# The long convolution's spectral products, ordered by feature tile instead of by spectrum half

## The reference

```python
def two_sided_fft_conv(u, h_fwd, h_bwd, bias):
    L = u.shape[1]
    kern = jnp.concatenate([h_fwd, jnp.zeros((1, h_fwd.shape[1]), F32), h_bwd[:0:-1]], axis=0)
    spec = jnp.fft.rfft(uf, n=2 * L, axis=1) * jnp.fft.rfft(kern, n=2 * L, axis=0)[None]
    y = jnp.fft.irfft(spec, n=2 * L, axis=1)[:, :L]
    return (y + uf * bias.astype(F32)).astype(u.dtype)

def hyena_mixer(h, ...):
    u = centred_depthwise_conv(h @ w_in + b_in, short_w, short_b)
    v, x1, x2 = jnp.split(u, 3, axis=-1)
    z = x1 * two_sided_fft_conv(v, filt[:, 0, 0], filt[:, 0, 1], filt_bias[0])
    z = x2 * two_sided_fft_conv(z, filt[:, 1, 0], filt[:, 1, 1], filt_bias[1])
    return z @ w_out + b_out
```

## Time and profile before

| | us |
|---|---|
| median of 3 runs | 3072.62 |
| the profiled execution's time | 3072.21 |
| its span, from the first to the last instruction | 3070.4 |
| TensorE busy | 2749.7 (90%) |
| VectorE busy | 1200.4 (39%) |
| ScalarE busy | 683.9 (22%) |

### The profile page before, as it was taken

The page is one execution under the profiler, slowest core; times in us unless marked ns, Lnnn a source line. Parts: engine busy times, 40 slices in busy tenths (PEclk is TensorE's granted clock), DMA queues, the critical chain, the costliest instruction groups (busy, mean ns, idle before and its releaser), DMA issues. The chain is left out here.

```text
span 3070.4 us, 37233 instructions
## 1 busy us (share of the span) xinstructions
PE 2749.7 (90%) x15352; PEld 1686.8 (55%) x15352; DVE 1200.4 (39%) x2257; ACT 683.9 (22%) x1422; POOL 20.1 (1%) x27
## 2 busy tenths in 40 slices
PE   8888999998998989867699999999898977988887
PEld 7656687885576667655463344333576755222223
DVE  5455433334365746575620111121536543111113
ACT  4344233332110111100211111111316631101101
POOL 0000000000000000000000000000010000000000
PEclk9999899997999999978799999999898989999998
DMA  4430423234110101010249999999331034999996
GB/s 177 144 124 7 159 82 110 82 110 159 52 52 1 55 24 41 24 55 0 111 157 375 353 346 344 344 340 345 123 139 46 2 137 165 415 427 429 427 428 256
DMA packets 56137, 550.17 MB, mean 179 GB/s; under 512 B 8199, under 2 KB 18823, under 8 KB 23208
## 3 DMA queue, kind: packets, MB, share of 16 engines
q1 hardware_dynamic: 55976, 547.93, 45.9%
HBM read 545.81 MB, written 2.10 MB: 178 GB/s over the span
## 5 line engine op out<-in xcount | busy, mean ns | idle before, releaser
L2623 PE MATMUL experts_pg_l<-ring,moe_xe_l 128*64 128x512 f32 x1024 | 269.5, 604 | 43.1 <-DMA ring<-in_moe_gu 37.7
L2623 PE MATMUL experts_pu_l<-ring,moe_xe_l 128*64 128x512 f32 x1024 | 263.5, 592 | 0.0
L2815 DVE SCALAR_TENSOR_TENSOR residual<-experts_psc,mod,residual 128x512 f32<-128x512 f32 (+1 forms) x101 | 71.9, 715 | 449.1 <-PE experts_psc L2704 375.0
L2648 PE MATMUL experts_py_l<-ring,experts_turn_l 128*64 128x512 f32 x976 | 223.6, 600 | 24.3 <-DMA ring<-in_moe_down 23.0
L1820 PE MATMUL hyena_lat<-normed,ring 128*128 128x512 f32 x384 | 172.2, 602 | 8.5 <-PEq L415 7.2
L2623 PEld LDWEIGHTS experts_pg_l<-ring,moe_xe_l 128*64 128x64 f32 x1024 | 63.4, 136 | 170.3 <-issue 101.9
L2648 PEld LDWEIGHTS experts_py_l<-ring,experts_turn_l 128*64 128x64 f32 x976 | 66.6, 137 | 163.0 <-issue 122.5
L2623 PEld LDWEIGHTS experts_pu_l<-ring,moe_xe_l 128*64 128x64 f32 x1024 | 74.3, 137 | 145.5 <-issue 145.5
L1820 PEld LDWEIGHTS hyena_lat<-normed,ring 128*128 128x128 f32 x384 | 73.1, 192 | 94.3 <-issue 93.2
L2807 DVE TENSOR_TENSOR experts_y_low<-experts_py_l,experts_y_whole 64x512 fp32r<-64x512 f32 x64 | 44.1, 689 | 196.9 <-ACT experts_y_whole L2765 134.8
L2796 DVE SCALAR_TENSOR_TENSOR experts_hid_l<-experts_act_l,moe_gate_rows,experts_pu_l 128x512 f32<-128x512 f32 x32 | 23.9, 747 | 238.8 <-ACT experts_act_l L2748 238.8
(11 more groups left out here) (551 smaller groups left out, 4999.4 us busy)
## 6 DMA issues: line engine op xcount, KB each, us to landing
ring<-in_moe_gu SPq DMA_DIRECT2D x128, 2048.0 KB, 10.1
ring<-in_moe_down SPq DMA_DIRECT2D x61, 2048.0 KB, 10.0
ring<-in_ada_w SPq DMA_DIRECT2D x24, 2048.0 KB, 7.8
ring<-in_w_up SPq DMA_DIRECT2D x8, 2048.0 KB, 7.7
ring<-in_w_down SPq DMA_DIRECT2D x8, 2048.0 KB, 7.7
ring<-in_hy_w_in SPq DMA_DIRECT2D x4, 2048.0 KB, 8.1
ring<-in_w_in SPq DMA_DIRECT2D x3, 2048.0 KB, 15.0
hyena_win<-table_window SPq DMA_DIRECT2D x4, 1536.0 KB, 7.5
```

The lines of the kernel that those rows point to most:

```text
L2623: last = nc.tensor.matmul((pg_l, pu_l)[m][64 * half:64 * half + 64, :], xe_l[:, e, k, :], w[:, kk, m, FH * half:FH * (half + 1)], start=(k ...
L2648: last = nc.tensor.matmul(py_l[64 * half:64 * half + 64, :], turn_l[:, c, i, :], columns(c, FH * half, FH), start=(f == 0), stop=(f == KD ...
L2815: nc.vector.scalar_tensor_tensor(out=x[:, d, c0:c0 + n], in0=banks[bank][:, 0:n], scalar=gate[j][:, d:d + 1], in1=x[:, d, c0:c0 + n], op0= ...
```

## The change

`products` handles a tile of 128 features, both halves of the spectrum, and then that tile's four sums, before it goes on to the next tile. `combined` is raised once for each tile, and `back` waits for it once for each tile. The twelve products keep 768 elements each, now as 6 rows of 128 out of 256; the sums are 8 of 3 × 128 instead of 4 of 768.

```diff
--- before.py
+++ after.py
@@ -1754,7 +1754,7 @@
         even_kept = st.counter("hy_even_kept", 24 * TURNS)
         convolved = st.counter("hy_convolved", NP * TURNS)
         taps_made = st.counter("hy_taps_made", 12 * TURNS)
-        combined = st.counter("hy_combined", 2 * TURNS)
+        combined = st.counter("hy_combined", 4 * TURNS)
         gated = st.counter("hy_gated", 2 * TURNS)
         win_loaded = st.counter("hy_win_loaded", 32 * TURNS)
         tab_loaded = st.counter("hy_tab_loaded", 64)
@@ -1863,8 +1863,8 @@
                         last.then_inc(ip_done.handle, 1)
 
                 def back(it, o):
-                    pe.wait_ge(combined.handle, it * 2 + combined.at(o + 1))
                     for j in range(2):
+                        pe.wait_ge(combined.handle, it * 4 + combined.at(2 * o + j + 1))
                         bl, bc = take(it, "back", 2 * o + j)
                         for b, table, tiles, n in ((bl, tables["idft_l"], (0, 1), 256), (bc, tables["idft_c"], (2,), P)):
                             for par in range(2):
@@ -2045,21 +2045,22 @@
                         dve.wait_ge(taps_made.handle, it * 12 + taps_made.at(6 * o + t + 1))
 
                 def products(it, link, o):
-                    for s in range(2):
-                        A, B = flat(ab[:, 0, s]), flat(ab[:, 1, s])
-                        Pc, Qs = flat(pq[:, 0, s]), flat(pq[:, 1, s])
-                        p1, p2 = (t1, t2) if s == 0 else (t3, t4)
-                        nc.vector.tensor_tensor(p1[:], A, Pc, ALU.mult)
-                        link(nc.vector.tensor_tensor(p2[:], B, Qs, ALU.mult))
+
+                    for j in range(2):
+                        tile = slice(j * P, (j + 1) * P)
+                        A, B, Pc, Qs = [v[:, a].rearrange("p s f n -> p (s f) n")[:, :, tile] for v in (ab, pq) for a in range(2)]
+                        p1, p2 = [t[:].rearrange("p (f n) -> p f n", n=P) for t in ((t1, t2), (t3, t4))[j]]
+                        nc.vector.tensor_tensor(p1, A, Pc, ALU.mult)
+                        link(nc.vector.tensor_tensor(p2, B, Qs, ALU.mult))
                         nc.vector.tensor_tensor(A, A, Qs, ALU.mult)
                         link(nc.vector.tensor_tensor(B, B, Pc, ALU.mult))
                         link(nc.vector.tensor_tensor(B, A, B, ALU.add))
-                        link(nc.vector.tensor_tensor(A, p1[:], p2[:], ALU.subtract))
-                    lo, hi = [flat(ab[:, a, 0]) for a in range(2)], [flat(ab[:, a, 1]) for a in range(2)]
-                    nc.vector.tensor_tensor(flat(pq[:, 0, 0]), lo[0], hi[0], ALU.add)
-                    nc.vector.tensor_tensor(flat(pq[:, 0, 1]), lo[0], hi[0], ALU.subtract)
-                    nc.vector.tensor_tensor(flat(pq[:, 1, 0]), lo[1], hi[1], ALU.subtract)
-                    nc.vector.tensor_tensor(flat(pq[:, 1, 1]), lo[1], hi[1], ALU.add).then_inc(combined.handle, 1)
+                        link(nc.vector.tensor_tensor(A, p1, p2, ALU.subtract))
+                        lo, hi = [[ab[:, a, s, :, tile] for a in range(2)] for s in range(2)]
+                        nc.vector.tensor_tensor(pq[:, 0, 0, :, tile], lo[0], hi[0], ALU.add)
+                        nc.vector.tensor_tensor(pq[:, 0, 1, :, tile], lo[0], hi[0], ALU.subtract)
+                        nc.vector.tensor_tensor(pq[:, 1, 0, :, tile], lo[1], hi[1], ALU.subtract)
+                        nc.vector.tensor_tensor(pq[:, 1, 1, :, tile], lo[1], hi[1], ALU.add).then_inc(combined.handle, 1)
 
                 def gates(it, link, o):
                     for j in range(2):
```

## The result

The changed kernel takes 3043.11 us (median of 4 runs, 3041.84 to 3044.01), the kernel before 3073.32 us (4 runs) in the same comparison: a ratio of 0.990 with an interval of 0.9888 to 0.9911. The forecast was 3041.7 us, with 3036 to 3048.5 as its range.

The account below looks back on a forecast made before the run. TensorE is busy 90% of the span, so only its idle and slow-clock time can give much. Five block gains sum to 30.7 us, giving 3041.5 from the profiled 3072.2 or 3041.9 from the median: 3041.7 us, range 3036 to 3048.5.

Parts of the forecast that it names:

- Which blocks wait: Inverse transform, 8 places: 3 covered by projections (order 0, full turns), 5 on TensorE's path, waiting 50.9 us in all.
- When the tiles are ready: From the products' start T on VectorE: tile 0 at T + 7.72, tile 1 at T + 15.30; before, both at T + 15.02.
- the larger estimate: Four extra sums on VectorE at a fixed 0.15 us each: 0.6 us a block instead of 0.28, 1.6 us in all five.
- The runs of 128: VectorE's products with operands in six runs of 128 elements: no cost taken; the other end was 9 us in all.
- Rival 5: VectorE's tile 1 work slows while TensorE loads tile 0's weights from pq: at factor 2.2, 15 us lost, 3087; chance 0.01.
- The start of tile 0 in a full turn: Order 1: TensorE leaves projection 5 at T + 9.02, transforms tile 0 to T + 13.36, then waits 1.94 us for tile 1.
- The tail: Order 1: the output product follows 7.10 us after tile 1's transform starts, as before, with tile 1's gating covered.
- Tile 0 in the last turn: Transform starts at T + 7.72 at the lower clock, ends at T + 14.7 or T + 13.8, ahead of tile 1.
- The gain of a block, b − 0.28: Each waiting block gains tile 0's old transform time b less 0.28: 6.89, 5.56, 5.74, 6.73 and 5.82 us.
- Rival 2: The new gap slows tile 1 in all three full turns, costing 6.0 to 8.5 us: 3047.7 to 3050; chance 0.15.
- rival 1: Slow stretches vanish behind the shorter gaps, 4.4 us more gained: 3037.3; chance 0.12.
- The shift reaches the end: Later loads wait for the program and move with the stage, so the whole 30.7 us was taken.

Follow-up runs that it names:

- experiment 2: The changed kernel with order 0 of the three full turns put back to the old form of `products`: 3045.88 us, ratio 0.9911 to the kernel before.
- experiment 8: The changed kernel with one more unread 768-element VectorE operation ahead of tile 1's products in all 8 blocks: 3047.7 us, ratio 0.9905 to the kernel before.
- experiment 5: The changed kernel with 4 unread matmuls in the gap ahead of tile 1 in the full turns: 3039.69 us, ratio 0.9893 to the kernel before.
- 4: The changed kernel with the output product begun on gated tile 0 while VectorE gates tile 1: 3033.6 us, ratio 0.9871 to the kernel before.
- experiment 6: The changed kernel with unread matmuls ahead of tile 1, the output product and the last turn's taps transform: 3037.44 us, ratio 0.9885 to the kernel before.
- the first run of 7: The changed kernel with the output product begun early and unread matmuls ahead of tile 1 and the taps' transform: 3027.0 us, ratio 0.9849 to the kernel before.
- experiment 3: The kernel before with unread matmuls ahead of each inverse transform that waits: 3057.54 us, ratio 0.995 to the kernel before.

## Why the prediction was right

- *Which blocks wait.* Three covered, five on the path: the blocks of the two traces and experiment 2 show it, and in experiment 8 0.87 us more of VectorE's time move tile 1 by 0.88 us in the five and by nothing in the three.
- *When the tiles are ready.* Forecast T + 7.72 and T + 15.30; measured 7.72 and 15.30 in the last turn. In the full turns tile 1 starts at T + 15.38, 0.08 us later than its signal would allow by the last turn's figures; these are the 0.06 and 0.07 us by which the first and the third turn fell short. The eight sums cost 0.28 us a block, not the 0.6 of the larger estimate.
- *The runs of 128.* They cost nothing. The line of L2053 and those of the sums, ns min/median/max:

```profile
L2053 DVE TENSOR_TENSOR hyena_t<-hyena_ab,hyena_pq x16: 948/954/958, 865.8 to 1396.3; 128x768 f32<-128x768 f32 x16
...
L2060 DVE TENSOR_TENSOR hyena_pq<-hyena_ab x16: 558/559/559, 871.5 to 1402.0; 128x384 f32<-128x384 f32 x16
...
L2063 DVE TENSOR_TENSOR hyena_pq<-hyena_ab x16: 547/550/553, 872.9 to 1403.4; 128x384 f32<-128x384 f32 x16
```

  The sums take the 0.56 us that was read between the forms of 256 and 512 elements, 0.47 apart. Rival 5 (VectorE slowed while TensorE loads weights from pq) fell by the same rows: the products of tile 1 that run beside tile 0's transform take 0.95 to 0.96 us.
- *The start of tile 0 in a full turn.* Forecast T + 9.02, measured 8.85: the 3.62 us of the projection's last group is an end that overlaps the next group. The transform still ended at T + 13.36 as forecast (948.71 − 2.02 = 946.69), so the early start gave and cost nothing. The gap is 2.02 us, not 1.94, because tile 1 starts at T + 15.38.
- *The tail.* 7.10 us from tile 1 to the output product; measured 7.09 (948.71 to 955.80). Behind its wait tile 1's transform takes 4.61 us to its end (955.80 − 2.48 − 948.71), over the 4.5 that was named as a sign of being wrong. That bound was too tight: 0.1 us of it is the first group behind a wait (3.71 us against 3.62), not a slow clock.
- *Tile 0 in the last turn.* Forecast to end at T + 14.7 and T + 13.8. It ended at T + 15.3 in order 0, with no wait left ahead of tile 1, and at T + 15.1 in order 1 (0.20 us of wait): the slow stretch was longer than in the old rows, the slack of 0.6 us in order 0 was used up, and that it cost nothing is luck.
- *The gain of a block, b − 0.28.* Four of five came within 0.1 us. The one step that missed is the clock behind the new gap, taken as 0: in the second turn tile 1 ran 1.69 us longer. Rival 2 thus held in one turn of three, in both profiles of the changed kernel and in that of experiment 2. Against it two output products that had been slow ran at full speed, part of rival 1. The forecast was for such a mixture. Between the blocks 5.0 us were gained and as much lost; the loss, 1.7 us in the first turn and 3.4 in the second in the filters and projection 4, stood in no term of the forecast, so that the two cancel is luck.
- *The shift reaches the end.* Of the 28.7 us 25.7 did (30.4 less the 4.7 that came ahead of the convolution). The first products of the expert stage still started 32.9 us earlier (1545.04 against 1577.89), so the loads came with the program, as the earlier trace rows let expect. Of the 3.0 us some 0.6 went by 2303 us of the old trace (32.8 us of shift left there) and the rest behind it, mostly in the second expert feed-forward; the cause is open. The sum of 30.7 was therefore 2.0 us too high in the blocks, mainly by the slow tile 1. That the 3041.7 us came so near 3043.11 is in part luck: 4.7 us came from ahead of the convolution and 3.0 went behind it.
- The Trainium skill's rule of gaps over about 3 us ("TensorE: Matmul & The Clock Gate", "Why this matters for your kernels") would have kept the clock up behind 2.0 and 2.5 us. The trace disagrees: tile 1 behind 2.02 us took 5.40 us in the second turn, the output product behind 2.48 us 3.60 in experiment 5. Nor does length alone decide: behind 2.90 us in experiment 8 tile 1 was fast in all three full turns, and slow once, behind 2.39, in the last. What came before seems to matter. Five profiles have nothing in the gap ahead of tile 1 (both of the changed kernel, experiments 2, 4 and 8), so fifteen such gaps in full turns. Tile 1 was slow in three, and these are the three where the turn had already lost 3.4 us before it (69.2 us from order 0's T to order 1's; elsewhere 67.5 or 65.8, a loss of 1.7 or none). Why was not tried.

## What to carry to other kernels

Where one engine makes a whole result and the next waits for all of it, order the work by what the consumer takes first and signal each piece. The gain is at most the consumer's time for the first piece, and only in the places where the wait is really on the path: read each occurrence, since three of eight here were covered. A long wait may bring slow-clock time right behind it; a third of this gain was that. Then look at the next joint of the chain, where the same step may be open again.

## What was not expected of the hardware

TensorE's granted clock fell to the lower level (1.2 GHz) without a gap worth the name. In the changed kernel's first turn the filters (L1840) have one gap of 0.48 us; projection 4 behind them takes 8.83 us, and about 7.1 us before. Timeline, then (fields as under the result) two stretches of the changed kernel and the like one of the kernel before, where the clock did not fall:

```profile
893.76 4.88 PE L1840 MATMUL hyena_spec<-hyena_w,hyena_h 64*128 64x256 f32 x20
899.12 1.13 PE L1840 MATMUL hyena_spec<-hyena_w,hyena_h 64*128 64x256 f32 x4 [0.48 <-DVE hyena_ab L2043]
900.18 8.83 PE L1820 MATMUL hyena_lat<-normed,ring 128*128 128x512 f32 x16
```

```profile
894.00:900.00 6.00, 5.48 (x24) 4.01 (x23) 5.53 (x11) 0.00 (x0) 0.00 (x0) 1.00 0.00 0
900.00:904.00 4.00, 4.00 (x7) 1.65 (x6) 3.74 (x9) 0.00 (x0) 0.00 (x0) 0.57 0.00 0
...
898.00:905.00 7.00, 6.48 (x30) 4.71 (x29) 5.79 (x12) 0.00 (x0) 0.00 (x0) 1.00 0.00 0
```

The engine was busy 5.48 of the 6 us before the fall, with filter products that use 64 of its 128 rows. In the kernel before it was busy 6.48 of 7 us there, with the same products and the same 0.48 us gap, and the clock stayed up; so these alone do not decide it. That stretch was slow in 9 of the 12 profiles of this study and fast in 3 (the kernel before, experiment 6 and the first run of 7). It is not the change's doing: experiment 3, the same as the kernel before up to that place, was slow too. Whether the half-used rows have a part in it was not tried. It makes 1.7 us each time, one source of the spread between executions of the same kernel.
